# Seven of nine RMS norms of a two-layer trunk: how the inverse root reaches all partitions

## The reference

```python
def rmsnorm(x, g):
    y = xf * lax.rsqrt(jnp.mean(xf * xf, axis=-1, keepdims=True) + EPS)
    return (y * g).astype(x.dtype)

for i in range(DEPTH):                                     # DEPTH = 2
    x = x + 0.5 * swiglu(rmsnorm(x, norm_ff1[i]), ...)     # norm k = 0
    x = x + token_mixer(rmsnorm(x, norm_mix[i]), ...)      # norm k = 1
    x = x + 0.5 * swiglu(rmsnorm(x, norm_ff2[i]), ...)     # norm k = 2
    x = x + sigmoid(rmsnorm(x, norm_ple[i]) @ w_g) * (p[i] @ w_p)   # norm k = 3
return rmsnorm(x, norm_final)                              # the ninth
```

## Time and profile before

| | |
|---|---|
| time, median of 3 runs | 1181.16 us (1180.98 to 1181.28) |
| span of the profiled execution | 1179.5 us; no time of its own is given for it, and the runs' median stands 1.66 us above this span |
| TensorE busy | 1168.9 us (99% of the span) |
| VectorE busy | 814.0 us (69%) |
| ScalarE busy | 593.7 us (50%) |
| GpSimd busy | 122.8 us (10%) |
| chain that ended last | 98% TensorE |

### The profile page before, as it was taken

The page is one execution under the profiler, slowest core; times in us unless marked ns, Lnnn a source line. Parts: engine busy times, 40 slices in busy tenths (PEclk is TensorE's granted clock), DMA queues, the critical chain, the costliest instruction groups (busy, mean ns, idle before and its releaser), DMA issues.

```text
span 1179.5 us, 24037 instructions
## 1 busy us (share of the span) xinstructions
PE 1168.9 (99%) x10534; PEld 1144.7 (97%) x10534; DVE 814.0 (69%) x939; ACT 593.7 (50%) x669; POOL 122.8 (10%) x136
## 2 busy tenths in 40 slices
PE   9999999999999999999999999999999999999997
PEld 9999999999999999999999999999899999999996
DVE  5866555688978766655786665558798777666455
ACT  5544445555745544444554444447367455444443
POOL 2000001011512000001210000100133020000011
PEclk9999999999999999999999999999999999999998
DMA  7655555545445555555555555554635365555541
GB/s 288 235 203 188 193 201 177 184 156 202 145 149 207 190 188 206 183 204 187 179 202 194 194 199 184 197 203 139 214 140 169 118 235 203 184 204 186 186 172 36
DMA packets 33384, 218.87 MB, mean 186 GB/s; under 512 B 5184, under 2 KB 6016, under 8 KB 7296
## 3 DMA queue, kind: packets, MB, share of 16 engines
q1 hardware_dynamic: 33280, 217.34, 53.2%
HBM read 216.15 MB, written 1.05 MB: 184 GB/s over the span
## 4 chain that ended last, share of the span: by engine, by line
PE 98%; DVE 1%; DMA 1%; ACT 0%; issue 0%; POOL 0%; SPq 0%; POOLq 0%; DVEq 0%
PE psum L385 31%; PE psum L387 31%; PE psum L386 31%; PE psum L665 1%; PE psum L644 1%; DMA x_all<-in_x 1%; PE psum L517 0%; PE psum L578 0%; PE psum L628 0%; PE psum L699 0%; PE psum L424 0%; PE psum L710 0%; PE psum L613 0%; DVE gates L1671 0%; PE psum L733 0%
## 5 line engine op out<-in xcount | busy, mean ns | idle before, releaser
L1222 DVE TENSOR_TENSOR w_lo<-raw,w_hi 128x2048 fp32r<-128x2048 f32 x200 | 457.9, 2293 | 213.5 <-ACT w_hi L856 213.4
L856 ACT ACTIVATE w_hi<-raw 128x2048 fp32r<-128x2048 f32 x201 | 385.2, 1917 | 366.6 <-PE psum L387 360.8
L385 PE MATMUL psum<-hA_hi,w_hi 128*128 128x256 f32 x1360 | 377.9, 278 | 0.0
L386 PE MATMUL psum<-hA_hi,w_lo 128*128 128x256 f32 x1360 | 375.7, 276 | 0.0
L387 PE MATMUL psum<-hA_lo,w_hi 128*128 128x256 f32 x1360 | 375.7, 276 | 0.0
L385 PEld LDWEIGHTS psum<-hA_hi,w_hi 128*128 128x128 f32 x1360 | 255.4, 188 | 2.7 <-issue 2.7
L386 PEld LDWEIGHTS psum<-hA_hi,w_lo 128*128 128x128 f32 x1360 | 255.4, 188 | 0.0
L387 PEld LDWEIGHTS psum<-hA_lo,w_hi 128*128 128x128 f32 x1360 | 255.3, 188 | 0.0
L385 PE MATMUL psum<-hB_hi,w_hi 128*128 128x256 f32 x832 | 230.3, 277 | 1.1 <-DVE w_lo L1654 1.1
L386 PE MATMUL psum<-hB_hi,w_lo 128*128 128x256 f32 x832 | 229.7, 276 | 0.0
L387 PE MATMUL psum<-hB_lo,w_hi 128*128 128x256 f32 x832 | 229.7, 276 | 0.0
(11 more groups left out here) (182 smaller groups left out, 1226.0 us busy)
## 6 DMA issues: line engine op xcount, KB each, us to landing
raw<-in_weights SPq DMA_DIRECT2D x203, 1024.0 KB, 4.9
raw<-in_weights SPq DMA_DIRECT2D x2, 512.0 KB, 6.2
out<-gates SPq DMA_DIRECT2D x3, 256.0 KB, 2.2
x_all<-in_x SPq DMA_DIRECT2D x1, 520.0 KB, 3.9
x_all<-in_x SPq DMA_DIRECT2D x1, 512.0 KB, 6.2
relu<-in_p SPq DMA_DIRECT2D x2, 256.0 KB, 5.0
consts<-in_consts SPq DMA_DIRECT2D x1, 384.0 KB, 5.7
out<-gates SPq DMA_DIRECT2D x2, 128.0 KB, 2.3
```

Source lines behind the costliest of these rows:

```text
L385: pe.matmul(o, lh, rh, start=start, stop=False)
L386: pe.matmul(o, ll, rh, start=False, stop=False)
L856: act.activation(w_hi[:, s, :], raw[:, s, :], ACT.Copy).then_inc(hi_ready[s], 1)
L1222: dve.tensor_tensor(w_lo[:, s, :], raw[:, s, :], w_hi[:, s, :].bitcast(F32), ALU.subtract).then_inc(lo_ready[s], 1)
```

## The change

Norm k = 1 keeps the old way, since its consumers need `rstd` with tokens on partitions. For the other seven the steps 2 to 5 are replaced. The squares are scaled by 1/32 inside the activation, so that their sum is the mean. One float32 product, ones (128x128) times `total` (256 columns), puts the mean square on all partitions (`mean_everywhere`); ScalarE takes the root from PSUM into `total`, with EPS as a bias from a tile (`root`); VectorE takes the reciprocal into `rb` (`inverse_root`). GpSimd's power, VectorE's two or three small tiles and the two rounded spreads go. The product stands in the middle of q = 2 in every `ffn`, and in the middle of the chunk `PGATE` in `embed`. At the end, the square of the last tile is taken by VectorE in place of ScalarE, and the last two tiles are multiplied by gain and `rb` in one instruction.

```diff
+            def mean_everywhere(L, k, b):
+                pe.wait_ge(sq_added, of_norm(L, k, 4) + START)
+                pe.matmul(bank[b][:, 0:T], ones[:, :], total[:, :], start=True, stop=True).then_inc(rb_sum, 1)
...
                     if q == 2:
-                        token_sums(L, k, 4) if first else spread(L, k, 4)
-                    if q == 3 and first:
-                        spread(L, k, 4)
+                        mean_everywhere(L, k, 4)
...
-                token_sums(L, 3, 7)
...
-                        by_columns(s, bank[4 + i], hA).then_inc(chunk_done[s], 1)
+                        by_columns(s, bank[4 + i], hA, (0,))
+                        if i == 0:
+                            mean_everywhere(L, 3, 7)
+                        by_columns(s, bank[4 + i], hA, (1,)).then_inc(chunk_done[s], 1)
...
-                    if i == 0:
-                        spread(L, 3, 7)
...
-                for t in range(2):
-                    half = slice(t * P, (t + 1) * P)
-                    mm = pe.matmul(bank[4][:, T + t:T + t + 1], last_squared[:, c - 1, half] if c else total[:, half], ones[:, 0:1],
-                                   start=c == 0 and t == 0, stop=c == 2, skip_group_check=True)
-            mm.then_inc(sums_done, 1)
-            spread(L_N, 0, 4)
+                mm = pe.matmul(bank[4][:, 0:T], ones[:, :], last_squared[:, c - 1, :] if c else total[:, :], start=c == 0, stop=c == 2)
+            mm.then_inc(rb_sum, 1)
...
-            def take_rb(L, k, b):
+            def root(L, k, b):
                 act.wait_ge(rb_sum, L * 4 + k + 1)
+                act.activation(total[:, :], bank[b][:, 0:T], ACT.Sqrt, bias=eps[:, 0:1]).then_inc(rooted, 1)
...
                     if g == 0:
                         split(L, n + 4)
-                        take_rb(L, 2 * f, 4)
+                        root(L, 2 * f, 4)
...
+            def inverse_root(L, k):
+                dve.wait_ge(rooted, of_root(L, k))
+                dve.reciprocal(rb[:, :], total[:, :]).then_inc(rb_ready, 1)
+                dve.wait_ge(rb_ready, L * 4 + k + 1)
...
                     if g == 0:
                         split(L, n + 3)
-                        if L == 0 and f == 0:
-                            dve.wait_ge(const_landed, 16)
-                        mean_square(L, 2 * f, 4)
+                        inverse_root(L, 2 * f)
                         split(L, n + 4)
-                        dve.wait_ge(rb_ready, L * 4 + 2 * f + 1)
...
                 if last:
-                    mean_square(L, 4, 4)
+                    dve.wait_ge(x_done, L * 16 + 16)
+                    dve.scalar_tensor_tensor(out=last_squared[:, 1, :], in0=x[:, 7, :], scalar=ROOT * ROOT, in1=x[:, 7, :],
+                                             op0=ALU.mult, op1=ALU.mult).then_inc(last_squares, 1)
...
+            inverse_root(L_N, 0)
             for m in STORES:
                 n = m.stop - m.start
-                dve.tensor_tensor(final[:, m, :], final[:, m, :], bank[4][:, 0:T].unsqueeze(1).to_broadcast([P, n, T]), ALU.mult
+                if n == 1:
+                    dve.scalar_tensor_tensor(out=final[:, m.start, :], in0=x[:, m.start, :], scalar=gains[:, 4, m], in1=rb[:, :],
+                                             op0=ALU.mult, op1=ALU.mult).then_inc(out_ready, 1)
+                    continue
+                dve.tensor_tensor(final[:, m, :], final[:, m, :], rb[:, :].unsqueeze(1).to_broadcast([P, n, T]), ALU.mult
                                   ).then_inc(out_ready, 1)
```

More of the change, by code:

```diff
@@ L15 @@
 EPS = 1e-6
+ROOT = 1 / 32
 N_FF = 11
@@ L149, in hybrid_trunk @@
         gbias = sb("gbias", [P, 2])
+        eps = sb("eps", [P, 1])
         wi = sb("wi", [P, 2, 8])
@@ L234, in hybrid_trunk @@
         rb_sum = sem("rb_sum")
+        rooted = sem("rooted")
         rb_ready = sem("rb_ready")
@@ L252, in hybrid_trunk @@
         last_squares = sem("last_squares")
-        final_scaled = sem("final_scaled")
         out_ready = sem("out_ready")
@@ L315, in of_norm, with of_root @@
             return (L * 4 + k) * 4 + pair
+        def of_root(L, k):
+            return L * 3 + max(k, 1)
         def piece(i):
@@ L425, in token_sums @@
                 mm.then_inc(sums_done, 1)
+            def mean_everywhere(L, k, b):
+                pe.wait_ge(sq_added, of_norm(L, k, 4) + START)
+                pe.matmul(bank[b][:, 0:T], ones[:, :], total[:, :], start=True, stop=True).then_inc(rb_sum, 1)
             def spread(L, k, b):
[L429 to L433, removed]
+                pe.wait_ge(diag_done, L + 1)
                 pe.matmul(bank[b][:, 0:T], ones_r[:, :], diag_hi[:, :, :].rearrange("p a t -> p (a t)"), start=True, stop=False)
@@ L440, in ffn @@
                 k = 2 * f
-                first = L == 0 and f == 0
                 s = operands(L, off) if f else turn(L, off)[0]
@@ L453, in ffn @@
                 for m in range(4):
-                    if m == 3 and not first:
-                        token_sums(L, k, 4)
                     if f == 0:
@@ L865, in squares @@
                 act.wait_ge(sq_added, of_norm(L, k, m) + START)
-                act.activation(squared[:, :, :], x[:, 2 * m:2 * m + 2, :], ACT.Square).then_inc(sq_done, 1)
+                act.activation(squared[:, :, :], x[:, 2 * m:2 * m + 2, :], ACT.Square, scale=ROOT).then_inc(sq_done, 1)
             def take_pair(L, k, m, h, squares_too=True):
@@ L925, in mix @@
                 split(L, MIX + 3)
-                take_rb(L, 1, 6)
+                take_rb(L, 6)
                 chunk_products(L, AV + 1)
@@ L1065, in embed @@
                 split(L, PROJ + 3)
-                take_rb(L, 3, 7)
+                root(L, 3, 7)
                 for i in range(3):
@@ L1080, in embed @@
                         squares(L, 4, 2)
+                    if last and c:
+                        continue
                     act.wait_ge(x_done if c else tile_added, (L * 16 + 16) if c else (L + 1))
                     if last:
-                        act.activation(last_squared[:, c, :], x[:, 6 + c, :], ACT.Square).then_inc(last_squares, 1)
+                        act.activation(last_squared[:, c, :], x[:, 6 + c, :], ACT.Square, scale=ROOT).then_inc(last_squares, 1)
                     else:
@@ L1087, in embed @@
                 if last:
-                    for c in range(2):
-                        act.activation(final[:, 6 + c, :], x[:, 6 + c, :], ACT.Copy, scale=gains[:, 4, 6 + c:7 + c]).then_inc(final_scaled, 1)
+                    root(L_N, 0, 4)
                 else:
@@ L1150, in norm @@
                         pool.tensor_tensor(total[:, :], total[:, :], squared[:, 1, :], ALU.add).then_inc(sq_added, 1)
-                pool.wait_ge(mean_done, L * 4 + k + 1)
-                pool.tensor_tensor(rstd[:, :], mean[:, :], half_neg[:, 0:2], ALU.pow).then_inc(rstd_done, 1)
+                if k == 1:
+                    pool.wait_ge(mean_done, L + 1)
+                    pool.tensor_tensor(rstd[:, :], mean[:, :], half_neg[:, 0:2], ALU.pow).then_inc(rstd_done, 1)
+                elif pairs == 4:
+                    pool.wait_ge(rb_ready, L * 4 + k + 1)
             start_counts(pool, [sq_added])
             pool.memset(ones[:, :], 1.0).then_inc(ones_ready, 1)
+            pool.memset(eps[:, :], EPS)
             pool.memset(half_neg[:, :], -0.5).then_inc(half_ready, 1)
@@ L1256, in add_half, with mean_square @@
                                          ).then_inc(x_done, 1)
[L1258 to L1262, removed]
+            def mean_square(L, b):
+                dve.wait_ge(sums_done, L + 1)
+                dve.tensor_scalar(mean[:, :], bank[b][:, T:T + 2], EPS, None, ALU.add).then_inc(mean_done, 1)
+                dve.wait_ge(rstd_done, L + 1)
+                dve.wait_ge(const_landed, 16)
                 roots = rstd[:, :].unsqueeze(2).to_broadcast([P, 2, P])
-                if L * 4 + k == L_N * 4:
-                    dve.tensor_tensor(diag[:, :, :], both(ident), roots, ALU.mult).then_inc(diag_done, 1)
-                    return
                 dve.tensor_tensor(diag_hi[:, :, :], both(ident), roots, ALU.mult).then_inc(diag_rounded, 1)
-                dve.wait_ge(diag_rounded, L * 4 + k + 1)
+                dve.wait_ge(diag_rounded, L + 1)
                 for t in range(2):
@@ L1311, in ffn @@
                         rest_pair(L, k, m, h)
-                        if m == 3:
-                            mean_square(L, k, 6 if f == 0 else 7)
+                        if m == 3 and f == 0:
+                            mean_square(L, 6)
                     split(L, n + 3)
@@ L1348, in mix @@
                 split(L, MIX + 3)
-                dve.wait_ge(rstd_done, L * 4 + 2)
+                dve.wait_ge(rstd_done, L + 1)
                 for r, factor in ((r_eighth, 0.125), (r_less, -0.125), (r_half, 0.5)):
@@ L1582, in embed @@
                 split(L, PROJ + 3)
-                dve.wait_ge(rb_ready, L * 4 + 4)
```

(1 more changed line is left out.)

6 lines of the change are left out of this document (3 added, 3 removed).

## The result

The changed kernel took 1205.51 us (median of five, 1205.43 to 1205.65) beside 1181.28 for the kernel before (five, 1180.98 to 1181.35). The ratio is 1.0206, interval 1.0193 to 1.0218. That is 24.2 us slower, where 3 us faster was forecast. The span is 1203.6 us.

What follows compares the result with a forecast made beforehand. It took TensorE, fed for 99% of the span, to bound the kernel. Its stream's -1.4 us and the tail's -1.6 made -3.0, so 1181.16 became 1178.1 us; the range was 1177.1 to 1181.5.

Steps and rivals of the forecast that it cites:

- GpSimd's power, VectorE's diagonals and the extra memset: Small steps removed or added on GpSimd and VectorE: they lie beside other work and count for nothing.
- A: The reciprocal is slow by column, in the tail and the first norm; 1181.9 us, halfway 1179.8; chance 0.24.
- B: The tail's table load waits with the root for TensorE's sum; 1179.3 us; chance 0.10 with the drain.
- C: The float32 product is dear in TensorE's stream, 1.05 us in each of six norms; 1182.3 us; chance 0.06.
- Sums and spreads out, product in: TensorE's stream, six norms: removing sums and spreads gives -4.2 us, the float32 product adds 2.8; together -1.4 us.
- Ten more table loads: ScalarE's ten further table loads, 1.28 us each, were costed at nothing.
- The drain that the Trainium skill adds: Some 1.38 us more for each ScalarE table load, 2.66 us a switch; by it the estimate would be 1178.7.
- T: VectorE's reciprocal on 256 columns in the tail: 0.42 us taken, upper bound 2.8.
- the tail's gain: From the last x tile to the last store: -1.78 us until the final multiplications start, +0.14 in them, -1.6 us.
- A's upper end: Reciprocal 2.4 us longer than assumed: tail +0.8, about 1.3 us of waiting in the first norm; 1181.9 us.
- The prediction's own chain: First norm: root, reciprocal, VectorE's split, gate, Silu, rounding lead to chunk 5's `w_lo` ending at 35.6, 1 us earlier.
- Two of its signs of being wrong: In the changed trace: a reciprocal over 1 us, a load beginning after the sum, a wait at chunk 4 or 5.

Runs made afterwards that it cites:

- e1: The changed kernel with `eps` in the unused words of `mean`'s row, so that no tile moves; 1179.93 us, ratio 0.9989.
- e2: The kernel before with an unused 64-byte tile where the change declares `eps`; 1207.17 us, ratio 1.0219.
- e9: The kernel before with only the last norm's part of the change, `eps` in `mean`'s row; 1181.05 us, ratio 0.9998.
- e5: The kernel before with only `hB` and `hid` moved 64 bytes further; 1207.26 us, ratio 1.0220.
- e7: The kernel before with only `hB` and `hid` moved 64 bytes back; 1203.45 us, ratio 1.0188.
- e12: The kernel before plus 16 stretches of 168 rounded products behind its last output, reading `hA` 0 to 448 bytes further on; one profiled run, 1496.79 us.
- e4: The kernel before with an unused 128-byte tile ahead of `hB` and `hid`; four runs, 1189.94, 1190.03, 1197.42 and 1197.45 us, ratio 1.0116.
- e6: The kernel before with only `hB` and `hid` moved 256 bytes further; 1181.2 us, ratio 0.9999.
- e3: The kernel before with everything in the SBUF moved 64 bytes further; 1181.11 us, ratio 0.9998.
- e8: The kernel before with `w_lo` moved 64 bytes further, moving tiles and `w_hi` fixed; 1221.03 us, ratio 1.0337.
- e10: e1 with the float32 product of `mean_everywhere` issued twice in six norms; 1182.0 us, 2.07 above e1.

## Why the prediction was wrong

**The step that failed** is half a sentence: "GpSimd's power, VectorE's diagonals and the extra memset lie beside other work: nothing." The memset itself costs nothing to be seen in e1. What was not priced is the tile that it fills. The part took `eps` as an instruction and not as a declaration, and a declaration moves every tile behind it. e2 prices exactly that at 25.9 us, e1 takes it away. None of the rivals A, B and C had it. Each of them kept to the view that opened the prediction, in which TensorE's stream can only be interrupted: "the rounded products start 0.113 us apart". That figure was treated as a constant of the product, and it is a property of the layout.

The trace of the kernel before could not have priced this, since its products with `hA`, `hB` and `hid` all run at the full pace. But its code gave notice: it holds tiles that nobody reads, and two constants with PLACE in their names.

**The other steps**, in e1, where they can be read without the 25.6 us:

- Sums and spreads out, product in: -1.4 was forecast, -1.1 measured (the last start of a product, e1 against the kernel before). The product came at 0.43 (0.46 taken), which would give -1.6; the 0.4 us for which TensorE waits in the first norm makes it -1.2. Rival C is out: 0.43, far under its 0.9. Its row, L431 with 1.22 us at granted clock 0.50, was the clock's: the same form in the tail of the changed kernel (L834) takes 0.70, at granted clock 1.00 in the window 1195.10:1195.80.
- Ten more table loads: at nothing, and right. The load went ahead of the wait also in the tail, where it ended at 1194.99 and the root started at 1195.86, 0.04 after TensorE's sum. B is out. The drain that the Trainium skill adds ("ScalarE: Activation LUTs", "What ACT_TABLE_LOAD costs") doesn't show: at 404.25 the root starts 0.02 us after its load.
- The reciprocal: a size was off, T = 0.42 against 1.75. This is rival A's mechanism, nearer to its halfway than to its bound. It took nearly all of the tail's gain (-1.6 forecast, -0.25 between e9's medians) and 0.4 us in the first norm, not the 1.3 of A's upper end. The prediction's own chain gives that wait: `w_lo` of chunk 5 at 35.6 + 1.33 = 36.9 where it is due at 36.4. (At A's upper end the same chain gives 38.0, not the 37.8 on record.) Two of its signs of being wrong came true here, apart from the layout: a reciprocal over 1 us, and a wait at chunk 5. The evidence against A, "on 2 columns it costs what others do", was worthless: 6.3 ns a column is 12 ns on two. The Trainium skill ("VectorE: DVE Perf Modes", "First, the fixed hardware budget") speaks of a repeat count of 8, from which the estimate was 2.3 us. Against it stands a slope of 6.3 ns a column; other operations have (415 - 150) / 254 = 1.0. The direction was the Trainium skill's; the measured factor is 6.
- The sum of these, 1179.93, lies inside the range on record, 1.8 above the value. Rival A's halfway, 1179.8, is nearer to it than the forecast is.

**What stays open.** The runs show that the place of the moving tile against `w_hi` and `w_lo` sets the pace, with a period of 256 bytes in the moving tile's place, and that TensorE alone suffices. They don't show what inside the memory or the engine does it. `w_hi` was never moved by itself. Modulo 256, `w_lo` stands at 0 and `w_hi` at 128: the loss at +64 (e2, e5) is with the moving tile at `w_hi`'s place, the one at -64 (e7) at `w_lo`'s. That the places must not coincide is not the whole rule, though, since in e12 the stretch at 128 bytes stands 64 bytes from both and is slow. Nor do the runs explain e4: in e12 the stretch at 128 bytes is slow throughout, while e4, with the same distance, ran its first FFN at full pace and came out at two different times.

## What to carry to other kernels

A new tile is a change to the address of every tile declared behind it. Where TensorE bounds a kernel, put a small new tile into the unused end of an existing row (e1), and after any change count the products in a window that the change should not touch: 885 against 842 told here what no wait did. An operation seen only on two columns has no price by column; bound it by both, and let the bound weigh more than the likeness.

## What the hardware showed that was not expected

- Rounded products of 128x256 run 0.1133 us apart or 0.1183 to 0.1191 apart, at the same granted clock 1.00 and with no wait in the trace. With nothing else changed, the moving tile's start address decides (e12). The fast places found, modulo 512: `w_hi` at 384, `w_lo` at 0 and the moving tile at 64 or 320 (e6, e12), or all moved together by 64 (e3).
- A product is slowed also when only its neighbour's weights move (e8): 39.7 us over 203 x 48 = 9744 products, 4.1 ns each on average.
- VectorE's reciprocal takes 1.75 us on 128x256, 0.16 us on 128x2.
- A float32 product of 128x256 between rounded ones costs 0.43 us, a second one straight behind it 0.42 (e10, timeline); rounded ones cost 0.113.
